# A sum over finished product tiles issued two row chunks earlier on TensorE

## The reference

```python
x = x + gt_m * rms_norm(y, g_post_mix[l])           # y: output of the sublayer
h = rms_norm(x, g_pre_ffn[l]) * (1.0 + sc_f) + sh_f
y = conv_ffn(h, w_up[l], conv_w[l], conv_b[l], w_down[l])
x = x + gt_f * rms_norm(y, g_post_ffn[l])
```

## Time and profile before

| | |
|---|---|
| median of 3 runs | 1585.51 us (1582.42 to 1586.15) |
| the profiled execution, its own time | 1586.39 us |
| its span in the profile | 1584.6 us |
| PE busy (matmuls) | 1508.6 us, 95% |
| PEld busy (weight loads) | 1255.7 us, 79% |
| POOL, ACT, DVE busy | 715.3, 648.2, 585.3 us |
| mean granted TensorE clock | 0.968 of full speed |
| DMA | 162.75 MB, 103 GB/s |

### The profile page before, as it was taken

How to read it: one execution, slowest core, us unless ns; L and a number is a source line. 1 busy time by engine, 2 the same in 40 slices (tenths; PEclk the granted TensorE clock), 3 DMA queues, 4 the chain that set the end, 5 groups by cost and what they waited for, 6 DMA issues and landing times.

```text
span 1584.6 us, 19944 instructions
## 1 busy us (share of the span) xinstructions
PE 1508.6 (95%) x7726; PEld 1255.7 (79%) x7726; DVE 585.3 (37%) x877; ACT 648.2 (41%) x941; POOL 715.3 (45%) x608
## 2 busy tenths in 40 slices
PE   9899997999999999999978989999899999999996
PEld 7698976788888888888945688888787888887885
DVE  3765452633333110523044410433225665654002
ACT  2453353644444332323254443543334554554331
POOL 1375303544545544554412255345535555545452
PEclk7899998999999999999999989999999999999998
DMA  8564125333232223233201123223311333232321
GB/s 360 190 255 168 42 72 110 89 106 104 81 106 90 88 77 97 100 107 133 94 24 57 58 100 123 67 64 109 107 54 53 108 104 101 84 99 87 96 76 67
DMA packets 28492, 162.75 MB, mean 103 GB/s; under 512 B 4584, under 2 KB 4840, under 8 KB 13704
## 3 DMA queue, kind: packets, MB, share of 16 engines
q1 hardware_dynamic: 24960, 151.05, 27.8%
q10 hardware_dynamic: 3464, 10.74, 2.7%
HBM read 157.04 MB, written 4.74 MB: 102 GB/s over the span
## 4 chain that ended last, share of the span: by engine, by line
PE 69%; issue 10%; POOL 9%; DVE 6%; ACT 3%; DMA 2%; POOLq 0%; ACTq 0%; SPq 0%; DVEq 0%
PE ps L1690 58%; POOL WL L789 7%; PE ps L1656 2%; DMA raw<-w_up_dram 1%; PE ps L1636 1%; POOL WL L751 1%; DMA xT<-x_dram 1%; PE ps L1934 1%; PE ps L1915 1%; DVE dl L1319 1%; ACT S L1119 1%; PE ps L1627 1%; DVE S L1567 1%; PE ps L1608 1%; DVE xT L1313 1%
## 5 line engine op out<-in xcount | busy, mean ns | idle before, releaser
L751 POOL TENSOR_TENSOR WL<-raw,WH 128x512 fp32r<-128x512 f32 (+2 forms) x344 | 369.9, 1103 | 529.0 <-ACT WH L869 528.9
L1690 PE MATMUL ps<-hH,WH 128*128 128x512 f32 x1024 | 405.4, 396 | 2.8 <-DVE hL L1445 1.9
L1690 PE MATMUL ps<-hH,WL 128*128 128x512 f32 x1024 | 399.9, 390 | 0.0
L1690 PE MATMUL ps<-hL,WH 128*128 128x512 f32 x1024 | 399.7, 390 | 0.0
L789 POOL TENSOR_TENSOR WL<-raw,WH 128x512 fp32r<-128x512 f32 x176 | 246.7, 1433 | 221.9 <-ACT WH L1027 221.9
L869 ACT ACTIVATE WH<-raw 128x1024 fp32r<-128x1024 f32 (+3 forms) x172 | 147.9, 885 | 233.9 <-PE ps L1690 226.2
L1690 PEld LDWEIGHTS ps<-hH,WH 128*128 128x128 f32 x1024 | 192.7, 188 | 47.1 <-issue 6.8
L1690 PEld LDWEIGHTS ps<-hH,WL 128*128 128x128 f32 x1024 | 192.8, 188 | 40.5
L1690 PEld LDWEIGHTS ps<-hL,WH 128*128 128x128 f32 x1024 | 192.8, 188 | 38.8
L1690 PE MATMUL ps<-hidH,WH 128*128 128x512 f32 x352 | 137.9, 392 | 1.1 <-POOL WL L789 1.1
L1690 PE MATMUL ps<-hidL,WH 128*128 128x512 f32 x352 | 137.0, 389 | 0.0
(11 more groups left out here) (292 smaller groups left out, 2307.4 us busy)
## 6 DMA issues: line engine op xcount, KB each, us to landing
raw<-w_up_dram SPq DMA_DIRECT2D x44, 1024.0 KB, 4.9
raw<-w_in_dram SPq DMA_DIRECT2D x36, 1024.0 KB, 4.9
adaw<-w_ada_dram SPq DMA_DIRECT2D x22, 1024.0 KB, 6.9
raw<-w_down_dram SPq DMA_DIRECT2D x16, 768.0 KB, 4.1
raw<-w_down_dram SPq DMA_DIRECT2D x16, 640.0 KB, 3.9
xT<-x_dram ACTq DMA_DIRECT2D x2, 2048.0 KB, 11.0
raw<-w_mem_kv_dram SPq DMA_DIRECT2D x4, 1024.0 KB, 4.7
raw<-w_out_dram SPq DMA_DIRECT2D x4, 1024.0 KB, 4.8
```

Source lines behind the costliest of these rows:

```text
L751: pool.tensor_tensor(WL[:, d % 2, ks, cols], raw[:, d % 2, ks, cols], WH[:, d % 2, ks, cols].bitcast(F32), ALU.subtract).then_inc(lo_done, 1)
L1690: mm = pe.matmul(out, lhs[x], rhs[y], start=(first and i == 0), stop=(last and i == 2))
```

## The change

```diff
@@ -508,7 +508,8 @@
                 if last:
                     nk = unit_source(d)[1]
-                    out += [("seg", d, 1, 0, nk - 2), ("sums", n, k), ("seg", d, 1, nk - 2, nk), ("square", n, k + 1)]
+                    out += [("seg", d, 1, 0, nk - 2), ("sums", n, k)] + [("cross_sums", n, 0)] * (n != N_POSTF2)
+                    out += [("seg", d, 1, nk - 2, nk), ("square", n, k + 1)]
                     return out
@@ -522,7 +523,7 @@
         def boundary(n, nxt):
             v = STAGE[n][1] - 1
-            return [("cross_sums", n, 0), ("sums", n, KD - 1), ("cross_sums", n, 1), ("split", v + 2, 0),
+            return [("sums", n, KD - 1), ("cross_sums", n, 1), ("split", v + 2, 0),
                     ("root_y", n), ("spread_y", n), ("root_x", n), ("warm", 2, v + 1), ("spread_x", n),
                     ("evac_y", n, KD - 1), ("warm", 4, v + 1), ("blend", n, nxt)]
```

## The result

The changed kernel takes 1588.65 us (median of 11 runs, 1585.96 to 1590.92), the kernel before beside it 1584.76 us (11 runs, 1581.22 to 1586.15). The ratio is 1.003 with a 95% interval of 1.0021 to 1.0039, that is 3.3 to 6.2 us slower. The forecast was 1588.5 us and +3.0 us (0.19%). That the time itself came out within 0.2 us is in part luck. The forecast started from 1585.5 us, the median of three runs, and over 11 runs the kernel before has 1584.76: the start was 0.7 too high and the step 0.9 too low.

A forecast was written before the change was run, and what follows sets the result against it. TensorE's queue was taken as the bound. Boundary terms of +1.19, +0.90 and +0.90 gave about +3.0 us on the 1585.5 us median, so 1588.5 us, with a range of 1585.4 to 1592.0 us.

The forecast's parts named there:

- What bounds: Whole kernel: TensorE's queue is the bound; a microsecond of matmuls added in a dense stretch costs a microsecond.
- The old place: Behind the last products, the group fills TensorE's wait for tile 7's square: moving it gains 0.0 us, 0.56 at half clock.
- A group in the stream: Ahead of the last six products, the moved group costs 0.90 us at full clock, 1.71 at half.
- No wait for VectorE's add: Second and third boundary: the moved group does not wait for VectorE to add tile 6; 0.5 us slack at the second.
- First boundary +1.19: First boundary at half clock: 0.04 wait plus 1.71 for the group less 0.56 gained behind the products.
- rival B: First boundary: the clock comes back, saving 1.6 us or 1.2 more; sum +1.4 or +0.2; chance 0.07.
- Rival A: Second and third boundary: the clock falls earlier, 2.8 us at each; +8.6 in all, 1594.1 us; chance 0.12.
- Rival C: First boundary: a late weight load behind it swallows the shift; only +1.8 remains, 1587.3 us; chance 0.10.
- Rival D: All three boundaries: the path behind the products shortens and the group in front hides in a wait; 1582.0 us; chance 0.03.
- The sum +3.0: All three boundaries together: +1.19 at the first, +0.90 at the second, +0.90 at the third; chance 0.68.
- the low bound of 0.79: Group ahead of the last products at full clock: lowest price, if the slower first product behind it is paid once.

The follow-up runs named there:

- left_out: The kernel before without the moved cross-sum group at the three boundaries (that part of the sum is missing); ratio 1.0006 to the kernel before.
- after_again: The changed kernel, unchanged, measured a second time against the kernel before: 1588.83 against 1582.55 us, ratio 1.0042.
- after_third: The changed kernel, unchanged, run once more for its profile: one execution, 1589.05 us.
- hole_filled: The changed kernel with one group with no use in the moved group's old place; ratio 1.0041 to the kernel before.
- only_first: The kernel before with the group moved at the first boundary alone; ratio 1.0018 to the kernel before.
- front_four: The changed kernel with three more groups with no use behind the moved one, ahead of the last products; 1607.48 against 1583.91 us, ratio 1.0147 to the kernel before.
- dense_after: The changed kernel with 34 products with no use where the first stage waits for its weights; 1585.47 us, ratio 1.0012 to the kernel before.
- dense_delay: The kernel before, nothing moved, with 9 products with no use in the second stage; 1586.20 against 1583.24 us, ratio 1.0021.
- dense_before: The kernel before with 34 products with no use where the first stage waits for its weights; 1581.18 against 1584.97 us, ratio 0.9979.
- best: The kernel before with those 34 products, and VectorE adding the fourth stage's squares of tiles 0 to 6; 1575.29 against 1582.55 us, ratio 0.9953.

## Why the prediction was right, and where it was not

- What bounds: right. The change is on TensorE's queue, and its groups come out in the time.
- The old place hides the group, 0.0 us at full clock and 0.56 at half: right, 0.00 and 0.59 (left_out).
- A group in the stream costs 0.90 us: right. The changed kernel's three profiles have six boundaries at the second and third place, and four of them are 0.88 longer. No wait for VectorE's add there: right.
- First boundary +1.19: right in size where the clock stays at half (+1.10 in after_again and after_third). But the forecast took that for the one case and gave rival B, the return of the clock, 0.07. It was there in one of the changed kernel's three profiles, and in those of hole_filled and only_first, and takes 0.53 us away instead. This is the step that failed: not the mechanism of rival B, which the prediction had, but the reason to rule it out, that the same six products at the same pace had not brought the clock back before. The price of rival B was right as well: 15.96 - 14.33 = 1.63, forecast 1.6. With it the forecast would have been +1.4 us, further from what was measured.
- Rival A, the earlier fall: as a mechanism it is shown, by front_four at more than the forecast price (2.8 us at each boundary; measured 4.6 and 4.2, since the groups in front slowed too: at the second boundary they took 4.20 instead of 2.70 us). dense_after is in line with it. In the changed kernel no fall came ahead of the sums of tile 7 at these two boundaries. One inside the second cross sum took 0.44 us, once in six boundaries; the 0.10 of another wasn't traced.
- Rival C: out. No new wait for a load showed in the first boundary's profiles, and from the next sublayer's first product to the second boundary's sums of tile 6 it takes 365.91 us before and 365.84 and 365.90 after (after_again): the shift is passed on whole. Rival D: out by left_out.
- The sum +3.0: the boundaries give +2.9 in the execution without the clock's return. The medians gave +3.9 and, in the second measurement, +6.3, and the intervals begin at +3.3 and +4.4. What the boundaries don't hold, some 1 to 3 us, stays open; the sum had no term for it. Of its terms, only the low bound of 0.79 doesn't follow from its rows (0.90 less 0.48 - 0.39 is 0.81), and nothing hangs on that. In three profiles of the changed kernel the stretch between the second and third boundary took 533.9 to 534.5 us, in two of before 532.7 and 530.2. That the shift of the path brings this about is argued only; dense_delay didn't show it, and kernels with nothing moved reach 535.04.

## What to carry to other kernels

Before a small step is moved ahead on the engine that bounds, look at what stands in its old place: a group that fills the wait for another engine is free, and the same group in the dense stream costs all of its length. Read both prices from the timeline, start to start, and ask what a first wait of its own adds. The same rule points the other way: small matmuls that stand in a dense stream are worth moving into such a hole, with an idle engine adding up first what they would have summed one by one, which here gave 6.4 us. And where the difference is a few us, don't price it from one profile: the share of half clock alone moves this kernel by as much.

## What the runs showed of the hardware

- The clock's fall and return fall to different places from execution to execution of one kernel: the first boundary of the changed kernel took 14.33, 15.96 and 15.96 us. A single profile misprices a change of 1 us next to such a place.
- In front_four the clock fell during the three groups with no use, while TensorE had one matmul after the other in the profile (PE busy 3.08 of 3.08 us at clock 0.50), and the six products behind them ran at half, 0.43 us a step. So here the profile's busy time didn't say whether the clock holds. The Trainium skill (TensorE: Matmul & The Clock Gate, section on the HAM clock gate) speaks of a monitor that sets the clock by how busy the array has been; going by the busy row, one would have expected no fall here, and the measurement decides.
- A group of 4 of these small matmuls takes 0.88 to 0.92 us from start to start at full clock and 1.71 to 1.73 at half, ahead of the last products and behind them.
- Dense products with no use during a wait of 8.8 us kept the clock up through the products behind it and made the kernel faster (dense_before: 0.9979, 0.9968 to 0.9989). Not in every execution: in best, with the same 34 products, the clock fell at the start of the last six.
